# Gated units fed from the residual stream: norm's inverse root at eviction, operand split during the preceding projection

## What is computed

```python
def rms_norm(x, g):
    xf = x.astype(jnp.float32)
    y = xf * lax.rsqrt(jnp.mean(xf * xf, axis=-1, keepdims=True) + RMS_EPS)
    return (y * g.astype(jnp.float32)).astype(x.dtype)
...
def modulated_norm(x, g, shift, scale):
    return rmsnorm(x, g) * (1 + scale) + shift

def swiglu_2(h, w1, w3, w2):
    return (jax.nn.silu(h @ w1) * (h @ w3)) @ w2
...
        x = x + y
        x = x + swiglu(rms_norm(x, norm_ffn[i]), ffn_w_gu[i], ffn_w_down[i])
...
        x = x + 0.5 * mx[2] * swiglu_2(modulated_norm(x, norm_g[l, 0], mx[0], mx[1]), *ffn1)
```

## Time and profile before

| what | us |
|---|---|
| runs, median of three | 4511.63 |
| lowest and highest | 4498.15, 4531.02 |
| span of the profiled execution | 4510.3 |
| PE busy | 4057.2 (90%) |
| DVE busy | 1601.6 (36%) |
| ACT busy | 1937.0 (43%) |
| POOL busy | 2664.8 (59%) |

### The profile page before, as it was taken

How to read it: one execution, slowest core, us unless ns; L and a number is a source line. 1 busy time by engine, 2 the same in 40 slices (tenths; PEclk the granted TensorE clock), 3 DMA queues, 4 the chain that set the end, 5 groups by cost and what they waited for, 6 DMA issues and landing times.

```text
span 4510.3 us, 94606 instructions
## 1 busy us (share of the span) xinstructions
PE 4057.2 (90%) x36305; PEld 3703.4 (82%) x36305; DVE 1601.6 (36%) x3002; ACT 1937.0 (43%) x2635; POOL 2664.8 (59%) x1186
## 2 busy tenths in 40 slices
PE   5899798899799889799999987999789999998799
PEld 5555798899589745499999977999689899987799
DVE  4533313413721453321212185215832212138421
ACT  3211445554344321154545454544545455446453
POOL 4001586486268500178778755777378787864576
PEclk8999899999899899999999998999899999999899
DMA  5345464365147334456556634555256565643454
GB/s 155 101 131 148 124 191 145 103 193 149 38 144 203 115 111 131 117 159 196 160 168 195 176 108 131 168 162 164 70 160 192 158 193 167 189 139 100 132 168 145
DMA packets 1177129, 664.73 MB, mean 147 GB/s; under 512 B 30141, under 2 KB 1138441, under 8 KB 1176743
## 3 DMA queue, kind: packets, MB, share of 16 engines
q1 hardware_dynamic: 1176871, 661.06, 50.7%
HBM read 659.92 MB, written 1.05 MB: 147 GB/s over the span
## 4 chain that ended last, share of the span: by engine, by line
PE 71%; issue 13%; POOL 7%; DVE 5%; ACT 2%; SPq 1%; DMA 1%; POOLq 0%; DVEq 0%; ACTq 0%
PE bank L638 54%; POOL wlo L541 7%; PE bank L967 6%; PE bank L718 2%; PE bank L617 1%; PE bank L1065 1%; PE bank L1059 1%; PE bank L801 1%; PE bank L1036 1%; DVE RSTD L724 1%; DVE W L740 1%; PE bank L874 1%; PE bank L1067 1%; PE bank L1042 0%; DVE AL L696 0%
## 5 line engine op out<-in xcount | busy, mean ns | idle before, releaser
L541 POOL TENSOR_TENSOR wlo<-raw,whi 128x1024 fp32r<-128x1024 f32 (+3 forms) x1182 | 2664.6, 2271 | 1821.4 <-ACT whi L551 1814.0
L638 PE MATMUL bank<-AH,whi 128*128 128x256 f32 x6320 | 1804.9, 286 | 193.9 <-DVE AL L696 104.9
L638 PE MATMUL bank<-AL,whi 128*128 128x256 f32 x6320 | 1787.2, 283 | 0.0
L638 PE MATMUL bank<-AH,wlo 128*128 128x256 f32 x6320 | 1785.4, 282 | 0.0
L551 ACT ACTIVATE whi<-raw 128x1024 fp32r<-128x1024 f32 (+3 forms) x1182 | 1173.2, 995 | 1162.7 <-PE bank L638 1010.2
L638 PEld LDWEIGHTS bank<-AH,whi 128*128 128x128 f32 x6320 | 1223.3, 194 | 212.7 <-issue 181.6
L638 PEld LDWEIGHTS bank<-AL,whi 128*128 128x128 f32 x6320 | 1225.6, 194 | 0.1
L638 PEld LDWEIGHTS bank<-AH,wlo 128*128 128x128 f32 x6320 | 1224.2, 194 | 0.0
L638 PE MATMUL bank<-HH,wlo 128*128 128x256 f32 x1936 | 537.0, 277 | 0.0
L638 PE MATMUL bank<-HH,whi 128*128 128x256 f32 x1936 | 537.0, 277 | 0.0
L638 PE MATMUL bank<-HL,whi 128*128 128x256 f32 x1936 | 537.0, 277 | 0.0
(11 more groups left out here) (334 smaller groups left out, 4281.5 us busy)
## 6 DMA issues: line engine op xcount, KB each, us to landing
raw<-in_ffn_w SPq DMA_DIRECT2D x420, 512.0 KB, 3.9
raw<-in_w_in SPq DMA_DIRECT2D x182, 512.0 KB, 3.8
raw<-in_ffn_w_gu SPq DMA_DIRECT2D x176, 512.0 KB, 3.8
raw<-in_w_ada SPq DMA_DIRECT2D x144, 512.0 KB, 4.1
raw<-in_ffn_w_down SPq DMA_DIRECT2D x64, 512.0 KB, 4.2
raw<-in_rw_w_rkv SPq DMA_DIRECT2D x48, 512.0 KB, 4.2
raw<-in_ffn_w SPq DMA_DIRECT2D x56, 384.0 KB, 3.4
raw<-in_ds_w_in SPq DMA_DIRECT2D x28, 512.0 KB, 3.7
```

Of the source, the lines that this page charges most:

```text
L541: pool.tensor_tensor(wlo[slot][:, 0:n], raw[slot][:, 0:n], whi[slot][:, 0:n], ALU.subtract).then_inc(lo_ready, 1)
L638: mm = pe.matmul(ps[:, 0:o.shape[2]], w, o[:, k0 + c, :], start=tile not in started and c == n == 0, stop=last_panel and c == nk - 1 and n ...
```

## The change

- The inverse root of a token is left out of the operand. The operand is gain times stream; `up` and gate results are multiplied by the inverse root when DVE empties their banks, into banks 5 and 6, and the silu reads from there.
- The operand of the next unit is made while the projection that writes the stream still runs, chunk by chunk behind each residual (`dve_residual`, `act_high_parts`, `dve_low_parts`), and DVE also sums the squares there into one tile for seven chunks and one for the last. Two products by ones stand behind the unit's first panel instead of eight in front of it. Where the stream being written is not the unit's own (f10c and f11c, behind f10x.down and f11x.down), chunks do not wait for the residual.
- A shift can't be added any more before the inverse root is known. It becomes two more moving columns of the operand's high part (its own high part and the rest; AH's chunks are 260 columns apart, 258 are streamed), whose results DVE adds to an offset of one column.
- The operands of output projections get tiles of their own (OUTH, OUTL).
- The context's turning moves into `ffn3.down` (behind tiles 0 and 1), its load ahead of it on SP. Modulation tables are kept for both layers and made between `up` and `down` of ffn3 and f20x; the lambda product comes behind tile 2.

The core of the diff; names and gains passed along are left out:

```diff
 
 
-        A = (v3(AH), v3(AL))
+        AH_v, AL_v = v3(AH, AW), v3(AL)
+        A = (AH_v[:, :, 0:S], AL_v)
+        A_SHIFTED = (AH_v[:, :, 0:S + 2], AL_v)
+        OUT = (v3(OUTH), v3(OUTL))
         HID = (v3(HH), v3(HL))
         BR = (v3(BRH), v3(BRL))
...
+
+        NORM_AFTER = {n: (X, True) for n in ("ffn0.down", "ffn1.down", "ffn2.down", "f21x.down")}
+        NORM_AFTER |= {n: (CTX, True) for n in ("f10c.down", "f11c.down")}
         NORM_AFTER |= {n: (X, False) for n in ("f20c.down", "mix1c.v")}
+        SPLIT_AFTER = {"rw0.out": "ffn0", "sb.out": "ffn1", "ds.out": "ffn2", "rw3.out": "ffn3", "ffn3.down": "f10x",
+                       "f10x.down": "f10c", "mix0c.o": "f20c", "mix0x.o": "f20x", "f20x.down": "f11x",
+                       "f11x.down": "f11c", "mix1x.o": "f21x"}
 
         def steps_of(eng, g, per, step, peel=False, last_straight=False):
...
                     else:
                         act_round(act, g, q)
+                    if then:
+                        then(s, j, k)
+                if split_for:
+                    own_stream = FFN[split_for].after_own
+                    if own_stream and s > 0:
+                        act.wait_ge(bank_free, g.t0 + s)
+                    act_high_parts(act, split_for, s if own_stream else s + 1)
...
+        def act_high_parts(act, name, until):
+
+            f = FFN[name]
+            for c in range(high_made[0], until):
+                act.activation(AH_v[:, c, 0:S], f.x[:, c * S:(c + 1) * S], ACT.Copy, scale=f.gain(c)).then_inc(hi_part, 1)
+            high_made[0] = max(high_made[0], until)
+
+        def dve_low_parts(dve, name, until):
+
+            f = FFN[name]
+            for c in range(low_made[0], until):
+                dve.wait_ge(hi_part, after(dve, hi_part))
+                dve.scalar_tensor_tensor(AL_v[:, c, :], f.x[:, c * S:(c + 1) * S], f.gain(c), AH_v[:, c, 0:S],
+                                         ALU.mult, ALU.subtract).then_inc(operand_ready, 1)
+            low_made[0] = max(low_made[0], until)
+
+        def dve_shift_columns(dve, name):
+
+            f = FFN[name]
+            if f.shift is None:
+                return
+            m = f.shift.unsqueeze(2)
+            dve.tensor_copy(AH_v[:, :, S:S + 1], m).then_inc(dve_step, 1)
+            dve.wait_ge(dve_step, after(dve, dve_step))
+            dve.tensor_tensor(AH_v[:, :, S + 1:S + 2], m, AH_v[:, :, S:S + 1], ALU.subtract)
+
+        def dve_partial_square(dve, name, c):
+
+            xc = FFN[name].x[:, c * S:(c + 1) * S]
+            dst = SQSUM if c == 0 else SQLAST if c == C - 1 else SQ
+            op = dve.tensor_tensor(dst[:, :], xc, xc, ALU.mult)
+            if c == C - 1:
+                op.then_inc(partial_squares, 1)
+                return
+            op.then_inc(dve_step, 1)
+            dve.wait_ge(dve_step, after(dve, dve_step))
+            if c:
+                op = dve.tensor_tensor(SQSUM[:, :], SQSUM[:, :], SQ[:, :], ALU.add)
+                if c == C - 2:
+                    op.then_inc(partial_squares, 1)
+                else:
+                    op.then_inc(dve_step, 1)
+                    dve.wait_ge(dve_step, after(dve, dve_step))
+
+        def dve_residual(dve, name, x, gate=None, between=None):
+
+            g = G[name]
+            split_for = SPLIT_AFTER.get(name)
+            if not split_for:
+                dve_tiles(dve, name, take_residual(dve, x, gate))
+                return
+            tile = dve_tiles(dve, name, take_residual(dve, x, gate), by_hand=True)
+            own = FFN[split_for].after_own
+            for s in range(g.steps):
+                tile(s)
+                if s == 0:
+                    dve_shift_columns(dve, split_for)
+                if own:
+                    dve.wait_ge(bank_free, g.t0 + s + 1)
+                dve_partial_square(dve, split_for, s)
+                dve_low_parts(dve, split_for, s if own else s + 1)
+                if between and s in between:
+                    between[s]()
+            dve.wait_ge(bank_free, tiles_of(name))
 
         def act_squares(act, x, until):
...
 
-            hi, lo = dst or (AH, AL)
-            n = src.shape[1]
-            dve.tensor_copy(hi[:, 0:n], src[:, :]).then_inc(dve_step, 1)
-            dve.wait_ge(dve_step, after(dve, dve_step))
-            dve.tensor_tensor(lo[:, 0:n], src[:, :], hi[:, 0:n], ALU.subtract).then_inc(operand_ready, 1)
+            hi, lo = dst or A
+            n = src.shape[1] // S
+            src = src[:, :].rearrange("p (c t) -> p c t", t=S)
+            dve.tensor_copy(hi[:, 0:n], src).then_inc(dve_step, 1)
+            dve.wait_ge(dve_step, after(dve, dve_step))
+            dve.tensor_tensor(lo[:, 0:n], src, hi[:, 0:n], ALU.subtract).then_inc(operand_ready, 1)
             dve.wait_ge(operand_ready, after(dve, operand_ready))
...
+        def act_ffn(act, name):
+            f = FFN[name]
+            act_high_parts(act, name, C)
+            high_made[0] = 0
 
             def gate(s, j, k):
 
-                if k == 0:
-                    n = after(act, hidden_ready)
-                    if n is not None:
-                        act.wait_ge(hidden_ready, n)
-                    g = G[f"{name}.up"]
-                    ps = bank[(g.t0 + j * g.tiles) % RING]
-                    act.activation(silu[j % 2][:, :], ps[:, 0:S], ACT.Silu).then_inc(silu_ready, 1)
-            gate.per = {hidden_ready: 2}
-            act_panels(act, f"{name}.up", gate)
-            act_panels(act, f"{name}.down")
+                if k == 0 and isinstance(s, int) and s == 0:
+                    act.wait_ge(sums_ready, after(act, sums_ready))
+                    act.activation(STD[:, :], bank[4][:, 0:S], ACT.Sqrt, bias=eps[:, 0:1], scale=1.0 / D).then_inc(std_ready, 1)
+                if k == 1:
+                    act.wait_ge(gate_ready, after(act, gate_ready))
+                    g_in = bank[6][:, (j % 2) * S:(j % 2 + 1) * S]
+                    if f.shift is None:
+                        op = act.activation(silu[j % 2][:, :], g_in, ACT.Silu)
+                    else:
+                        op = act.activation(silu[j % 2][:, :], g_in, ACT.Silu, bias=offset[:, j % 2:j % 2 + 1])
+                    op.then_inc(silu_ready, 1)
+            gate.per = {gate_ready: 2}
+            act_panels(act, f"{name}.up", then=gate)
 
         def pe_ffn(pe, name):
-            pe_norm(pe)
-            pe_panels(pe, f"{name}.up", chunked=True)
-            pe_panels(pe, f"{name}.down", chunked=True, chunk_ready=hidden_ready)
-
-        def dve_ffn(dve, name, x, gain, shift=None, out_gate=None):
-            dve_norm(dve, x, gain, W[7], shift)
-            hidden = bank[5][:, 0:S]
-
-            def take(s, j, banks):
-
+
+            def norm_sums():
+                for k, t in enumerate((SQSUM, SQLAST)):
+                    pe.wait_ge(partial_squares, after(pe, partial_squares))
+                    mm = pe.matmul(bank[4][:, 0:S], ones[:, :], t[:, :], start=k == 0, stop=k == 1)
+                mm.then_inc(sums_ready, 1)
+            pe_panels(pe, f"{name}.up", chunked=True, after_first=norm_sums)
+
+        def pe_ffn_down(pe, name, by_hand=False):
+            return pe_panels(pe, f"{name}.down", chunked=True, chunk_ready=hidden_ready, by_hand=by_hand)
+
+        def dve_ffn(dve, name):
+            f = FFN[name]
+            dve_low_parts(dve, name, C)
+            low_made[0] = 0
+            dve.wait_ge(operand_ready, after(dve, operand_ready, C))
+            dve.wait_ge(std_ready, after(dve, std_ready))
+            dve.reciprocal(RSTD[:, :], STD[:, :]).then_inc(dve_step, 1)
+            dve.wait_ge(dve_step, after(dve, dve_step))
+            hidden, up = bank[5][:, 0:S], bank[5][:, S:2 * S]
+            g = G[f"{name}.up"]
+
+            def step(s, j):
+
+                banks = [bank[(g.t0 + j * g.tiles + t) % RING] for t in range(g.tiles)]
+                b = j % 2
+                dve.wait_ge(panels_done, after(dve, panels_done))
+                if f.shift is not None:
+                    dve.tensor_reduce(offset[:, b:b + 1], banks[0][:, S:S + 2], AX_X, ALU.add)
+                dve.tensor_tensor(bank[6][:, b * S:(b + 1) * S], banks[0][:, 0:S], RSTD[:, :], ALU.mult).then_inc(gate_ready, 1)
+                dve.wait_ge(panels_done, after(dve, panels_done))
+                if f.shift is not None:
+                    dve.tensor_reduce(offset[:, 2:3], banks[1][:, S:S + 2], AX_X, ALU.add)
+                dve.tensor_tensor(up, banks[1][:, 0:S], RSTD[:, :], ALU.mult).then_inc(bank_free, 2)
+                dve.wait_ge(bank_free, after(dve, bank_free, 2))
                 dve.wait_ge(silu_ready, after(dve, silu_ready))
+                if f.shift is None:
+                    op = dve.tensor_tensor(hidden, up, silu[b][:, :], ALU.mult)
+                else:
+                    op = dve.scalar_tensor_tensor(hidden, up, offset[:, 2:3], silu[b][:, :], ALU.add, ALU.mult)
```

(90 more changed lines are left out.)

201 lines of the change are left out of this document (119 added, 82 removed).

## The result

| | before | changed |
|---|---|---|
| median of 20 runs, us | 4508.8 (4496.0 to 4554.5) | 4550.9 (4534.6 to 4562.6) |
| ratio, 95% interval | | 1.0075, 1.006 to 1.009 |
| span of the profiled execution, us | 4510.3 | 4553.7 |

I had forecast 4488 with a range up to 4540. The kernel became 0.75% slower, outside the range and on the other side.

What follows compares the result with a forecast made beforehand. TensorE, busy 90% of the span, was taken as the bound, losing time at eleven seams. From the profiled 4510.3 us, +15.3 - 42.6 + 4.1 gave 4487; with 1.3 for the median, 4488 us, range 4445 to 4540.

Steps and rivals of the forecast that it cites:

- the shifted columns: Seven gated units' up projections: 258 streamed columns in 4,928 products cost only their extra columns, +4.1 us.
- (b): Rival: the 258-column width tips 7,392 products to the slower pace, 4.44 ns each, 33 us; 4517 us, chance 0.14.
- Output projections: Seven seams behind output projections: new cost 87.1 us against 71.8 for the old, so +15.3 us.
- The walk through mix1x.o: In that output projection, DVE's SBUF-only steps wait behind POOL's pieces; DVE ends at 36.3 us, new seam 9.8 us.
- The clock term: After each seam behind an output projection, eight us run at clock 0.68, losing 2.2 us as the mean of seven.
- Down projections: Four seams behind down projections: DVE keeps up within tiles; 20.7 us in all against 63.3, so -42.6 us.
- I take no loss of clock for so short a stop: Seams behind down projections, 2.5 or 2.0 us: no clock loss after the restart, except 1.0 us in f20x's seam.
- the context's turning: In ffn3's down projection: PE stops 2.6 us after tile 1; the 16 transposes, 1.97 us, stay PE's work.
- At nothing: Up projections' per-tile DVE and ACT work hides under PE and costs nothing; uncovered, it would be 121 us.
- (a): Rival: DVE steps slip in beside POOL, each seam is 0.5 + 0.9 us; 4398 us, chance 0.12.
- (d): Rival: in four down projections a fourth DVE step per tile meets a POOL piece; +77 us, 4565, chance 0.06.
- (c): Rival: in seven output projections POOL also waits for DVE, up to 0.42 us per piece; +20 us, 4508, chance 0.10.

## Why the prediction was wrong

**The step that failed** is the one on the shifted columns: "I take the 4.1, as pure columns", and under it, that the two paces of the earlier trace rows were something to be kept in the range as luck ("that can fall otherwise, by -21 to +14"). Two rows lay there with the same work, the same clock and 4.44 ns between them, and I looked for the cause in nothing that the diff changes. The only line of it that touches every stage, AH's size, I costed at nothing without saying so. The pace is +86.4 us where I had +4.1, and the runs put it down to the places of AH and of what lies behind it; in the changed kernel as it is, the two columns themselves cost nothing. Rival (b), the width tipping the pace, had the right quantity but the wrong extent: priced for 7,392 products, it came for 24,900, by the layout. Taken alone and with the right places the width costs 41, not 33, so (b) would have been true as well, and a little dearer.

**Output projections** (+15.3 forecast, -3.7 measured at the seam). The walk through mix1x.o held nearly step by step. DVE there in the changed kernel:

```profile
4326.02 0.47 DVE L773 SCALAR_TENSOR_TENSOR X<-bank,mods,X 128x256 f32<-128x256 f32 x1
4326.53 2.21 DVE L636 TENSOR_TENSOR sq<-X 128x256 f32<-128x256 f32 x1
4328.77 0.43 DVE L643 TENSOR_TENSOR sq<-sq,sq 128x256 f32<-128x256 f32 x1
4329.23 2.52 DVE L618 SCALAR_TENSOR_TENSOR AL<-X,gains,AH 128x256 fp32r<-128x256 f32 x1
...
4347.49 0.87 DVE L618 SCALAR_TENSOR_TENSOR AL<-X,gains,AH 128x256 fp32r<-128x256 f32 x2
```

Seven steps of 2.2 to 2.5 us, then a lag that limits itself, and the end 34.6 us after the projection's first product (4313.74) where I had 36.3. POOL's pieces keep their period of 2.83 us up to the sixth and then stand apart, 2.25 us the first time; I had said from the fourth on. PE at the seam:

```profile
4340.15 0.28 PE L723 MATMUL bank<-AH,wlo 128*128 128x258 f32 x1
4345.06 0.58 PE L723 MATMUL bank<-AH,whi 128*128 128x258 f32 x1 [4.63 <-DVE AL L618]
...
4346.77 0.58 PE L723 MATMUL bank<-AH,whi 128*128 128x258 f32 x1 [0.70 <-DVE AL L618]
...
4349.48 1.91 PE L883 MATMUL bank<-sq,ones 128*128 128x256 f32 x4
```

The first panel is through 10.7 us after the projection's end, a seam of 8.0 instead of 9.8 (my own terms, 36.3 + 0.5 - 24.4, give 12.4 and not the 12.5 that I went on with). The clock term was too small: the eight us from the restart run at 0.50 (4345.00:4353.00 above), 4.0 us lost where I had put 2.2, and over the seven restarts 25.9 where I had 15.4. A part of that is no loss, as PE waits for chunks in it anyway. Over the seven the new seams cost 70.9 us with their clock against my 87.1, and the old ones 74.6 against 71.8. DVE's steps behind POOL were right as a mechanism; the size of the sum was a fifth too large, with the clock priced too low in it.

**Down projections** (-42.6 forecast, -43.5 measured): f10x 7.7 us against 8.5 forecast, f10c 4.6 against 2.9, f11x 5.1 against 6.4, f11c 2.9 against 2.9. The stops themselves are 2.4 us from start to start in f10x and f11x (idle 2.15) and 2.1 in f10c and f11c (idle 1.78), waiting for low parts:

```profile
2195.09 0.39 PE L723 MATMUL bank<-AH,whi 128*128 128x258 f32 x1 [2.15 <-DVE AL L618]
```

That the sum fits so well is luck in part. "I take no loss of clock for so short a stop" was wrong: in three of the four the eight us from the restart run at 0.79, 1.7 us lost each, 5.1 in all where I had 1.0. What made up for it is the context's turning, 2.7 us where I had 5.1, and a shorter seam at f11x. For f10c the clock is the whole difference to the forecast; f11c stopped for as long and kept its clock. The two, from their restarts:

```profile
2387.00:2395.00 8.00, 8.00 (x51) 7.64 (x52) 2.65 (x5) 4.91 (x5) 3.35 (x2) 0.79 0.50 144
3801.00:3809.00 8.00, 8.00 (x65) 7.89 (x66) 3.36 (x7) 6.53 (x7) 4.79 (x2) 1.00 0.50 146
```

**At nothing**: right for the up projections' tiles. From the 200th product to the last of an up projection no distance over 0.15 us is left in any of the eleven units.

**The other rivals.** (a) fell with the DVE rows above. (d) fell with the down projections: PE stands nowhere in them but for the context's turning (2.7 us in ffn3, in the 20.4) and 0.2 us in f20x. (c), that POOL waits for DVE too, is true in part: where POOL's piece begins under a running DVE step it takes some 0.2 us longer.

```profile
4320.38 2.41 POOL L550 TENSOR_TENSOR wlo<-raw,whi 128x1024 fp32r<-128x1024 f32 x1 [10.38 <-ACT whi L560]
4323.21 2.61 POOL L550 TENSOR_TENSOR wlo<-raw,whi 128x1024 fp32r<-128x1024 f32 x1 [0.43 <-ACT whi L560]
```

Over the kernel POOL is busy 16 us longer (2681.0 against 2664.8), and PE was not held back by it.

**What stays open**: at the right distance, what picks 113.3 or 117.8 for a stage. It isn't the stage: f10x is slow in the kernel before and fast in the one with moved hidden operands, ffn0 the other way round, with the same up projections. Between a quarter and two fifths of the products had the slow pace in the three profiles with 256 columns and old distances (about 25, 33 and 37%). In those three, where the pace changed, PE had just stood. Behind 258 columns it went from 118.9 to 113.3 with the first products of the down projection, without a stop. How the weights' and the moving operand's reads meet is not in the records, so the reason for the 256 bytes is open too. For the kernel before with a pitch of 260 columns and nothing else there is no time; the pad behind AH and the moved hidden operands stand in for it.

## What to carry to other kernels

Before costing a change at nothing, list every tile whose size or address it moves, and look whether the bound engine reads them: here 128 bytes behind one tile cost 77 us, more than the change brought in any form that was run. Where a trace shows the same instructions at two paces at the same clock, that is a cause not yet known, and it belongs to the rivals with the price of all instructions that could get it, not to the noise. And a DVE step with only SBUF operands beside a busy POOL can cost most of a POOL piece (2.2 to 2.5 us instead of 0.4 to 0.5 here): put it on ScalarE, or see that there is at most one for each piece.

## What the runs showed of the hardware

- A stream of weight load and product with 256 fp32r columns comes at 113.3 or 117.8 ns at full clock if the moving operand starts 64 bytes below the weights, modulo 256 (64 against 128, or 192 against 0). At the other distances tried (moved up by 32, 64, 128 and 192 bytes) stages had 117.8 to 120.0, never 113.3.
- With the operands at that distance, 258 columns in two products of three cost a step of 5.6 ns on the mean, from 113.3 to 118.9; up to 304 columns the mean was 118.9 to 133.3, not in order of width. All of these are multiples of 1.11 ns.
- The granted clock over the eight us from a restart: after idle times of 1.7 to 1.8 us it stayed 1.00 in some and was 0.79 in others (three of seven behind the output projections with ScalarE's squares; f10c and not f11c in the changed kernel), after 2.15 us 0.79 (f10x and f11x of the changed kernel), after 4.6 us with smaller stops behind it 0.50 to 0.68 (seven), after the old seams 0.57 to 0.80 (eleven, two of them in the earlier trace rows). So the length of the stop alone did not decide it.
